# A PEER kernel: the fourth block of 128 tokens by fetched expert rows, the late low halves of u on GpSimd

## The chip, the cores and the metric

The kernel runs on one core of one Trainium2 chip. The core has TensorE (PE, with its weight loads shown as PEld), VectorE (DVE), ScalarE (ACT), GpSimd (POOL) and SyncE (SP), which here only issues DMAs. The metric is the device time of one execution in microseconds. It was measured in three runs, and one more execution was profiled.

## The reference

512 tokens of width 1024, one layer, all in float32. A layer norm, an adaptive modulation (six vectors from `c @ ada_w + ada_b`), a mixer (windowed means and a gated linear recurrence) and a residual come first. Then PEER, a layer of 16384 experts, each with a row of `u` and a row of `v` of width 1024, from which every token picks 128:

```python
def peer(h, w_q, k1, k2, u, v):
    ...
    v1, i1 = lax.top_k(s1, PEER_TOPK)            # 16 of 128 keys, 8 heads
    v2, i2 = lax.top_k(s2, PEER_TOPK)
    ...
    vs, j = lax.top_k(cand, PEER_TOPK)           # 16 of the 256 sums
    e = i1[j // 16] * PEER_NKEYS + i2[j % 16]    # the expert's number
    g = jax.nn.softmax(vs, axis=-1)
    ...
        act = jax.nn.gelu(jnp.einsum('td,tkd->tk', xb, u[eb]))
        return jnp.einsum('tk,tkd->td', gb * act, v[eb])
```

The indexing in the line of `e` is shortened here. A gated residual and a last layer norm follow.

## The kernel before

**PEER is computed densely.** The experts are worked in 128 tiles of 128, for all 512 tokens. For a tile, *expert inputs* are `gelu(u . h)` of 128 experts by 512 tokens; they are multiplied by a gate array that is zero where a token did not pick the expert; then the *values*, gated inputs times `v`, are summed over all tiles into 512 x 1024 outputs. Every float32 product is made of three fast ones from a high and a low half of each operand (`thrice`, lines 1042, 1043 and 1044: high x high, low x high, high x low). ScalarE rounds the high halves (`u_hi`, `v_hi`, `w_hi`), and VectorE or GpSimd subtracts them for the low ones (`u_lo`, `v_lo`, `w_lo`). An input tile is 8 chunks of the width x 3 = 24 matmuls with 512 moving columns.

**The stages.** After the mixer (to some 310 us of the profile) come:
- the *rank stage*: VectorE runs `route`, the top-16 searches for each head (lines 1660 to 1720), while TensorE makes input tiles 0 to 27 (`T_RANK`), with low halves by GpSimd (`split_u`, line 619), between which GpSimd does the affine part of a layer norm (lines 570 and 573). At its end TensorE transposes the routing results (line 1238);
- the *scatter*: 32 steps (`STEPS`, TB x 2 x 4). In each VectorE makes two pairs of one-hot arrays (lines 1760 and 1766), TensorE multiplies them in float16 into gate columns (lines 1249 and 1251) which ScalarE evicts and SP stores to DRAM (`gates`). 20 input tiles (`T_SCATTER`) are made between, low halves by VectorE (line 1753);
- the *store stage*: 16 more input tiles (`T_STORE`) while the last gates are stored. VectorE multiplies the last two pieces of `ada_w` (10 and 11, `partial_modulation`, lines 1396 and 1399). Low halves are GpSimd's. These 64 early tiles are spilled to DRAM (`early`);
- the *late stage*: the values of all tiles and the 64 other input tiles. 30 groups (`group`, `NQ`) of four tiles each: two late input tiles (`late_inputs`, 48 matmuls) and, by Strassen-Winograd's scheme on 2 x 2 blocks, 7 products of 12 matmuls, 84 in all. VectorE makes the sums ahead of it (`value_sums`, `weight_sums`), multiplies by the gates (`weigh`, lines 1793 and 1801), makes low halves (`lo_v`, line 1806, and `lo_w`, line 1811), and adds the products from PSUM into accumulators (`add_up`, line 1816, 11 a group). GpSimd makes the low halves of u in halves of 512 (line 642), each after a wait for a VectorE operation that puts it beside an `add_up`. The last 8 tiles are summed in the 8 banks (`last_sums`);
- the *end*: residual, layer norm (lines 2002 to 2013) and the output DMA.

**What sets the order.** Each engine runs its own queue in the order written. They wait for each other through semaphores by count. SP issues nearly all DMAs in order; a load waits until its buffer is read, so a blocked issue holds those behind it. `u_raw` has four buffers, `u_hi` and `u_lo` two, `v_raw` and `w_raw` four.

## Time and profile before

| | us |
|---|---|
| runs, median (lowest, highest) | 1713.15 (1711.06, 1713.55) |
| profiled execution | 1714.83 |
| its span, first to last instruction | 1713.0 |
| PE busy | 1690.3 (99%) |
| DVE busy | 1533.3 (90%) |
| ACT busy | 770.2 (45%) |
| POOL busy | 392.2 (23%) |
| DMA | 293.22 MB, mean 171 GB/s |

Busy times are sums over the profiled span. They count neither waits nor the issue of DMAs, and matmuls are pipelined, so that their durations overlap: the time that one costs is the distance of the starts of two in a row. The TensorE clock granted was 0.99 of full speed over the span.

### The profile page before, as it was taken

Reading aid. Unit: us, or ns where it says so; the run is one execution under the profiler, and the core shown is the slowest. Engines: PE = TensorE matmul, PEld = TensorE weight load, DVE = VectorE, ACT = ScalarE, POOL = GpSimd, SP = SyncE. Lnnn points to the kernel's source line nnn. Section 1 sums busy time; section 2 is a strip of 40 time slices with the busy share of each in tenths; the row PEclk is TensorE's granted clock in tenths of the full one; section 3 lists DMA queues with packets and bytes.
Section 4 is the critical chain, followed back from the end, with each engine's and each line's share of the span. In section 5 each row is a group of like instructions: output and inputs, shape, how many; then the busy total and the mean of one; then the engine's idle time right before and its main releaser. Section 6 shows DMA issues by size and latency. Waiting matters only on the chain.

```text
span 1713.0 us, 23880 instructions
## 1 busy us (share of the span) xinstructions
PE 1690.3 (99%) x8162; PEld 1369.0 (80%) x8162; DVE 1533.3 (90%) x2332; ACT 770.2 (45%) x843; POOL 392.2 (23%) x248
## 2 busy tenths in 40 slices
PE   8999999999999999999999999999999999999998
PEld 6774688888888888888888888888888888888886
DVE  6988879999899991579999999999999999999998
ACT  1460633323388883344444443534444343444440
POOL 1000345474400003422122222212222122222210
PEclk7999999999999999999999999999999999999999
DMA  9544410245459999744445343444534345443441
GB/s 386 210 165 161 160 46 1 76 140 196 148 176 281 284 285 317 259 164 167 150 148 183 139 177 125 165 166 147 184 122 174 145 150 181 147 180 117 174 179 74
DMA packets 139448, 293.22 MB, mean 171 GB/s; under 512 B 8288, under 2 KB 76000, under 8 KB 136704
## 3 DMA queue, kind: packets, MB, share of 16 engines
q1 hardware_dynamic: 137680, 287.34, 48.0%
q0 software_dynamic: 1424, 4.85, 0.8%
q8 instruction: 34, 0.56, 0.1%
q10 hardware_dynamic: 288, 0.29, 0.1%
q14 instruction: 22, 0.18, 0.0%
HBM read 237.93 MB, written 54.53 MB: 171 GB/s over the span
## 4 chain that ended last, share of the span: by engine, by line
PE 64%; DVE 16%; issue 9%; DMA 6%; POOL 2%; SPq 1%; ACT 1%; DVEq 0%; POOLq 0%; ACTq 0%
PE bank L1042 19%; PE bank L1044 19%; PE bank L1043 19%; DMA w_raw<-early_dram 5%; DVE acc L1816 2%; PE bank L1249 2%; PE bank L1251 2%; DVE v_lo L1806 1%; POOL u_lo L642 1%; DVE u_raw L1840 1%; DVE v_sum L1843 1%; DVE w_raw L1793 1%; DVE arena L1399 1%; PE bank L1128 1%; PE bank L1183 1%
## 5 line engine op out<-in xcount | busy, mean ns | idle before, releaser
L1042 PE MATMUL bank<-h_hi,u_hi 128*128 128x512 f32 x1264 | 498.6, 394 | 1.7 <-POOL u_lo L619 1.7
L1044 PE MATMUL bank<-h_hi,u_lo 128*128 128x512 f32 x1264 | 492.9, 390 | 0.0
L1043 PE MATMUL bank<-h_lo,u_hi 128*128 128x512 f32 x1264 | 492.7, 390 | 0.0
L1042 PE MATMUL bank<-v_hi,w_hi 128*128 128x512 f32 x872 | 341.7, 392 | 1.5 <-DVE acc_p L1816 1.3
L1043 PE MATMUL bank<-v_lo,w_hi 128*128 128x512 f32 x872 | 339.5, 389 | 0.0
L1044 PE MATMUL bank<-v_hi,w_lo 128*128 128x512 f32 x872 | 339.4, 389 | 0.0
L642 POOL TENSOR_TENSOR u_lo<-u_raw,u_hi 128x512 fp32r<-128x512 f32 x120 | 156.1, 1302 | 622.1 <-DVE w_raw L1793 417.0
L1042 PEld LDWEIGHTS bank<-h_hi,u_hi 128*128 128x128 f32 x1264 | 237.6, 188 | 50.7 <-issue 2.0
L1044 PEld LDWEIGHTS bank<-h_hi,u_lo 128*128 128x128 f32 x1264 | 237.7, 188 | 50.4
L1043 PEld LDWEIGHTS bank<-h_lo,u_hi 128*128 128x128 f32 x1264 | 237.9, 188 | 49.0 <-issue 0.7
L1042 PEld LDWEIGHTS bank<-v_hi,w_hi 128*128 128x128 f32 x872 | 163.7, 188 | 42.9 <-DVE acc_p L1816 8.9
L1044 PEld LDWEIGHTS bank<-v_hi,w_lo 128*128 128x128 f32 x872 | 163.7, 188 | 34.3
L1043 PEld LDWEIGHTS bank<-v_lo,w_hi 128*128 128x128 f32 x872 | 163.7, 188 | 33.1
L619 POOL TENSOR_TENSOR u_lo<-u_raw,u_hi 128x1024 fp32r<-128x1024 f32 x45 | 113.5, 2523 | 309.0 <-ACT u_hi L823 309.0
L885 ACT ACTIVATE v_hi<-v_raw 128x2048 fp32r<-128x2048 f32 x62 | 118.5, 1912 | 116.9 <-PE bank L1044 116.9
L1806 DVE TENSOR_TENSOR v_lo<-v_raw,v_hi 128x2048 fp32r<-128x2048 f32 x62 | 152.9, 2466 | 12.5 <-DMA early_dram<-arena 6.3
L1816 DVE TENSOR_TENSOR acc<-acc,bank 128x512 f32<-128x512 f32 x240 | 153.3, 679 | 0.5 <-PE bank L1044 0.5
L912 ACT ACTIVATE w_raw<-bank 128x512 f32<-128x512 f32 x64 | 38.3, 599 | 226.9 <-PE bank L1044 134.8
L830 ACT ACTIVATE arena<-bank 128x512 f32<-128x512 f32 x64 | 38.9, 608 | 165.9 <-PE bank L1044 165.9
L889 ACT ACTIVATE w_hi<-w_raw 128x1024 fp32r<-128x1024 f32 x62 | 65.9, 1064 | 81.2 <-PE bank L1044 79.9
L1801 DVE TENSOR_TENSOR w_raw<-w_raw,gate_in 128x1024 f32<-128x1024 f32 x31 | 38.6, 1247 | 46.0 <-DMA w_raw<-early_dram 45.9
L1811 DVE TENSOR_TENSOR w_lo<-w_raw,w_hi 128x1024 fp32r<-128x1024 f32 x62 | 78.9, 1272 | 0.0
(259 smaller groups left out, 2383.1 us busy)
## 6 DMA issues: line engine op xcount, KB each, us to landing
u_raw<-ut_dram SPq DMA_DIRECT2D x128, 512.0 KB, 3.5
v_raw<-v_dram SPq DMA_DIRECT2D x128, 512.0 KB, 6.3
gate_in<-gates_dram SPq DMA_DIRECT2D x64, 512.0 KB, 5.1
...
```

Of the source, the lines that this page charges most:

```text
L619: pool.tensor_tensor(u_lo[:, c % GT], u_raw[:, c % RT], u_hi[:, c % GT].bitcast(F32), ALU.subtract).then_inc(s_ulo, 1)
L642: return pool.tensor_tensor(u_lo[:, j, k], u_raw[:, 2 + j, k], u_hi[:, j, k].bitcast(F32), ALU.subtract)
L830: act.activation(gelu_out[:, c % GT, :], bank[banks[c % GT]][:, :], ACT.Gelu_apprx_tanh).then_inc(s_act, 1)
L885: act.activation(slots(v_hi, a, b), made, ACT.Copy).then_inc(s_vhi, 1)
L889: act.activation(slots(w_hi, a, b), made, ACT.Copy).then_inc(s_whi, 1)
L1042: pe.matmul(out, a_hi, b_hi, start=(k == 0), stop=False)
L1043: pe.matmul(out, a_hi, b_lo, start=False, stop=False)
L1044: return pe.matmul(out, a_lo, b_hi, start=False, stop=(k == n - 1))
L1801: ve.tensor_tensor(made, made, gate_in[:, :, :, 0, :], ALU.mult).then_inc(s_w, 1)
L1806: ve.tensor_tensor(slots(v_lo, a, b), made, slots(v_hi, a, b).bitcast(F32), ALU.subtract).then_inc(s_vlo, 1)
L1811: ve.tensor_tensor(slots(w_lo, a, b), made, slots(w_hi, a, b).bitcast(F32), ALU.subtract).then_inc(s_wlo, 1)
L1816: ve.tensor_tensor(part, part, bank[b][:, :], ALU.add).then_inc(s_acc, 1)
```

## The change

**Tokens.** Only three of the four blocks of 128 tokens (`DENSE = 3`) are worked densely. An input tile has 384 moving columns (`SD`), the scatter 24 steps, the gates 6 stages (`NST`). The mixer and the routing are still done for all 512 tokens.

**Values.** Winograd's scheme goes. Each tile has 6 outputs (3 blocks x 2 halves of the width) x 3 = 18 matmuls of 512 columns, which accumulate in banks 0 to 5 over the whole late stage; there is no `add_up`. The loop goes by pairs of tiles: one late input tile, then 36 value matmuls; 60 pairs, then three input tiles, then two closing passes of 72 matmuls.

**The fourth block.** For each of the 128 picks GpSimd fetches one row per token by an indirect DMA (128 rows of 4 KB, 512 KB), of u for picks 0 to 127 and of v for 128 to 255, into six row buffers (`first_rows`, 2, and `quad`, 4). VectorE multiplies each with `h_nat`, the block's h in natural layout, and sums along the row; after a gelu and the gates (at pair 28) it multiplies the rows of v with the pick's weight and adds them into `picked`. 12 picks stand in the store stage, then four in each pair. `h_nat` comes from 16 small f32 matmuls in the store stage.

**Low halves.** In the store stage VectorE makes those of u (tiles 52 to 65), in the late stage GpSimd, whole (128x1024) and between its fetches.

**Early tiles.** Still 64, as 36 + 16 + 12. `ada_w` 10 is loaded ahead of the scatter, into `xt`; 11 after it, into `quad`.

```diff
+DENSE = TB - 1
+SD = DENSE * P
+XB = TB - 1
-STEPS = TB * 2 * 4
+STEPS = DENSE * 2 * 4
-T_TURN, T_RANK, T_SCATTER, T_STORE = 27, 28, 5 * TB, 16
+T_TURN, T_RANK, T_SCATTER, T_STORE = 35, 36, 16, 12
```

SyncE's queue in the store stage:

```diff
-                if s in LATE_ADA:
-                    sp.wait_ge(s_scmm, 4 + S // 4)
+                if s == LATE_ADA_AT:
+                    sp.wait_ge(s_scmm, 4 + SD // 4)
+                    sp.dma_start(late_ada[1], ada_w[11]).then_inc(s_late[1], 16)
```

GpSimd's new function and its late loop:

```diff
+            def fetch(n):
+                of, k = (u, v_rows)[n // PICKS], n % PICKS
+                if n >= NBUF:
+                    pool.wait_ge(s_used, n - NBUF + 1)
+                pool.indirect_dma_start(row_buf(n), None, of, bass.IndirectOffsetOnAxis(ap=pick_at[:, k:k + 1], axis=0)
+                                        ).then_inc(s_rows_of[n % NBUF], 16)
...
+            for c in range(-1, PER * LOOPS):
+                n = first + (c + 1) * SLOT_PAIRS
+                for m in range(n, n + SLOT_PAIRS // 2):
+                    if m < 2 * PICKS:
+                        fetch(m)
+                split_u(0, T_EARLY + c + 3)
+                for m in range(n + SLOT_PAIRS // 2, n + SLOT_PAIRS):
+                    if m < 2 * PICKS:
+                        fetch(m)
```

TensorE's late loop:

```diff
+            def pair(i, c):
+                expert_inputs(i, T_EARLY + c + 1, BANKS_SCATTER[(c + 1) % 2], i * RT + (T_EARLY + c))
+                pe.wait_ge(s_wlo, i * PER + (c + 1))
+                pe.wait_ge(s_vlo, i * PER + (c + 1))
+                for j in range(2):
+                    w_of, v_of = pair_of(c % 2, j)
+                    for t in range(DENSE):
+                        for half in range(2):
+                            mm = values(w_of, v_of, t, half, isinstance(i, int) and i + c + j == 0, False)
```

VectorE's picks, and their places in `prepare(c)`:

```diff
+            def picks(count):
+                for n in range(done[0], done[0] + count):
+                    k, rows_of = n % PICKS, row_buf(n)
+                    ve.wait_ge(s_rows_of[n % NBUF], 16 * (n // NBUF + 1))
...
+                        ve.scalar_tensor_tensor(out=rows_of, in0=rows_of, scalar=1.0, in1=h_nat[:, :], op0=ALU.mult,
+                                                op1=ALU.mult, accum_out=dots[:, k:k + 1]).then_inc(s_used, 1)
...
+                    ve.scalar_tensor_tensor(out=picked[:, :], in0=rows_of, scalar=pick_g[:, k:k + 1], in1=picked[:, :],
+                                            op0=ALU.mult, op1=ALU.add).then_inc(s_used, 1)
...
+                else:
+                    picks(one)
+                    lo_v(c + 1)
+                    picks(one)
+                weigh(c + 1)
+                picks(2 * one)
+                lo_w(c + 1)
```

**Orders, before and after.** GpSimd, from the end of its rank loop to the first group of the late stage, before (u_lo are low halves of u, xcount operations in a row):

```order
L628 COMPARE_AND_BRANCH
L619 TENSOR_TENSOR u_lo<-u_raw,u_hi 128x1024 x19
L659 MEMSET acc 128x2048
L642 TENSOR_TENSOR u_lo<-u_raw,u_hi 128x512 x4
L655 TENSOR_TENSOR w_lo<-row_b,w_hi 128x2x256
```

GpSimd in the late stage, after (L586 is `split_u`, L609 `fetch`):

```order
L609 DMA quad<-u_dram,pick_at 128x1024 x2
L609 DMA first_rows<-u_dram,pick_at 128x1024 x2
L586 TENSOR_TENSOR u_lo<-u_raw,u_hi 128x1024
L609 DMA quad<-u_dram,pick_at 128x1024 x4
L586 TENSOR_TENSOR u_lo<-u_raw,u_hi 128x1024
L609 DMA first_rows<-u_dram,pick_at 128x1024 x2
L609 DMA quad<-u_dram,pick_at 128x1024 x2
```

The whole low halves now stand between fetches, two ahead and two behind each.

VectorE in the store stage, before: the last low half of the scatter, then the two pieces of `ada_w` (L1396, L1399):

```order
L1753 TENSOR_TENSOR u_lo<-u_raw,u_hi 128x1024
L1396 TENSOR_SCALAR arena<-acc,sc 128x512
L1399 SCALAR_TENSOR_TENSOR arena<-acc,sc,arena 128x512 x7
L1863 MEMSET acc 128x2048
L1865 MEMSET row_g 128x1024
L1396 TENSOR_SCALAR arena<-arena,sc 128x512
L1399 SCALAR_TENSOR_TENSOR arena<-arena,sc 128x512 x7
L1414 TENSOR_TENSOR row_gate<-row_gate,bank 128x512 x2
L1870 MEMSET acc_p 128x512
```

The same place, after (L1645 is `split_u`, L1282 and L1285 are the pieces, piece 10 in `xt`, piece 11 in `quad`):

```order
L1645 TENSOR_TENSOR u_lo<-u_raw,u_hi 128x1024 x2
L1282 TENSOR_SCALAR arena<-xt,sc 128x512
L1285 SCALAR_TENSOR_TENSOR arena<-xt,sc,arena 128x512 x3
L1645 TENSOR_TENSOR u_lo<-u_raw,u_hi 128x1024
L1285 SCALAR_TENSOR_TENSOR arena<-xt,sc,arena 128x512 x4
L1746 MEMSET picked 128x1024
L1645 TENSOR_TENSOR u_lo<-u_raw,u_hi 128x1024
L1282 TENSOR_SCALAR arena<-quad,sc 128x512
L1285 SCALAR_TENSOR_TENSOR arena<-quad,sc,arena 128x512 x3
L1645 TENSOR_TENSOR u_lo<-u_raw,u_hi 128x1024
L1285 SCALAR_TENSOR_TENSOR arena<-quad,sc,arena 128x512 x4
L1645 TENSOR_TENSOR u_lo<-u_raw,u_hi 128x1024 x4
```

The low halves of u have moved here from GpSimd, and two of them stand between and behind the parts of piece 11.

VectorE in the first group of the late stage, before (L1840 to L1845 `value_sums`, L1829 to L1834 `weight_sums`):

```order
L1840 TENSOR_TENSOR u_raw<-v_raw 128x2x512
L1842 TENSOR_TENSOR v_raw<-v_raw 128x2x512
L1843 TENSOR_TENSOR v_sum<-v_raw,u_raw 128x1024
L1845 TENSOR_TENSOR u_raw<-v_raw,v_sum 128x2x512
L1793 TENSOR_TENSOR w_raw<-w_raw,gate_in 128x512
L1816 TENSOR_TENSOR acc<-acc,bank 128x512 x2
L1829 TENSOR_TENSOR row_b<-w_raw 128x2x256
L1831 TENSOR_TENSOR w_raw<-w_raw 128x2x256
L1832 TENSOR_TENSOR w_sum<-row_b,w_raw 128x512
L1834 TENSOR_TENSOR row_b<-w_raw,w_sum 128x2x256
L1816 TENSOR_TENSOR acc<-acc,bank 128x512 x2
L1806 TENSOR_TENSOR v_lo<-v_raw,v_hi 128x2x1024
```

The same stage, after (L1688 `lo_v`, L1707 a pick, L1683 `weigh`, L1694 `lo_w`), the first pair and the start of the next:

```order
L1707 SCALAR_TENSOR_TENSOR first_rows,dots<-first_rows,h_nat 128x1024
L1688 TENSOR_TENSOR v_lo<-v_raw,v_hi 128x2048
L1707 SCALAR_TENSOR_TENSOR first_rows,dots<-first_rows,h_nat 128x1024
L1683 TENSOR_TENSOR w_raw<-w_raw,gate_in 128x768
L1707 SCALAR_TENSOR_TENSOR quad,dots<-quad,h_nat 128x1024 x2
L1694 TENSOR_TENSOR w_lo<-w_raw,w_hi 128x2x384
L1707 SCALAR_TENSOR_TENSOR quad,dots<-quad,h_nat 128x1024
```

The sums and the operations that read the banks are gone; picks stand between what is left.

## Rows read from the trace of the kernel before

**Rows 1.** Busy time by stage: window, us; engine busy (instructions); PE clock; DMA share; GB/s.
```profile
310.00:464.00 154.00, 152.30 (x685) 126.29 (x686) 149.54 (x549) 50.27 (x64) 88.07 (x36) 0.99 0.43 146
472.00:643.00 171.00, 169.58 (x1485) 142.32 (x1485) 166.29 (x146) 150.52 (x165) 0.00 (x0) 1.00 0.85 258
643.00:742.00 99.00, 99.00 (x441) 81.31 (x439) 37.23 (x31) 35.37 (x43) 42.91 (x17) 1.00 0.78 273
742.00:1680.00 938.00, 936.54 (x4110) 769.25 (x4109) 882.72 (x933) 410.39 (x376) 196.64 (x152) 1.00 0.44 157
```

**Rows 2.** Timeline, late stage, TensorE and weight loads: start, duration, operation.
```profile
1188.31 0.39 PE L1044 MATMUL bank<-v_hi,w_lo 128*128 128x512 f32 x1
1188.54 0.39 PE L1042 MATMUL bank<-v_hi,w_hi 128*128 128x512 f32 x1
1188.54 0.19 PEld L1043 LDWEIGHTS bank<-v_lo,w_hi 128*128 128x128 f32 x1
```

**Rows 3.** Timeline, plain f32 matmuls of 512 and of 384 columns, TensorE.
```profile
179.73 7.11 PE L1128 MATMUL bank<-wbuf,arena 128*128 128x512 f32 x16
186.68 0.49 PE L1015 MATMUL bank<-cst 128*128 128x384 f32 x1
186.68 3.39 PE L1015 MATMUL bank<-cst 128*128 128x384 f32 x10
```

**Rows 4.** VectorE groups: operation, shapes xcount | busy us, mean ns | idle before.
```profile
L1806 DVE TENSOR_TENSOR v_lo<-u_raw,v_hi 128x2048 fp32r<-128x2048 f32 x29 | 66.1, 2279 | 0.0
L1811 DVE TENSOR_TENSOR w_lo<-w_raw,w_hi 128x1024 fp32r<-128x1024 f32 x62 | 78.9, 1272 | 0.0
L1801 DVE TENSOR_TENSOR w_raw<-w_raw,gate_in 128x1024 f32<-128x1024 f32 x31 | 38.6, 1247 | 46.0 <-DMA w_raw<-early_dram 45.9
L1992 DVE SCALAR_TENSOR_TENSOR u_raw<-u_raw,acc 128x1024 f32<-128x1024 f32 x3 | 3.6, 1221 | 0.0
```

**Rows 5.** GpSimd groups, then a DMA of its queue: KB each, us to landing.
```profile
L619 POOL TENSOR_TENSOR u_lo<-u_raw,u_hi 128x1024 fp32r<-128x1024 f32 x45 | 113.5, 2523 | 309.0 <-ACT u_hi L823 309.0
L553 POOL DMA_DIRECT2D row_b<-rows_dram x2 | 1.1, 538 | 0.0
gate_in<-rows_dram POOLq DMA_DIRECT2D x2, 512.0 KB, 4.9
```

**Rows 6.** Timeline of GpSimd, then of VectorE, rank stage.
```profile
357.42 2.47 POOL L619 TENSOR_TENSOR u_lo<-u_raw,u_hi 128x1024 fp32r<-128x1024 f32 x1 [0.68 <-ACT u_hi L823]
...
357.55 2.42 DVE L1703 SCALAR_TENSOR_TENSOR arena<-arena 128x64 f32<-128x64 uint32 x1
362.38 1.23 DVE L1707 TENSOR_TENSOR arena<-arena,cst 128x1024 f32<-128x1024 f32 x1
...
370.21 3.41 DVE L1712 TENSOR_TENSOR arena<-arena 128x1024 f32<-128x1024 f32 x1
```

**Rows 7.** Timeline of VectorE, one and a half scatter steps.
```profile
562.62 2.36 DVE L1766 TENSOR_TENSOR acc<-acc,arena 128x2048 f16<-128x2048 f16 x2
564.89 1.23 DVE L1753 TENSOR_TENSOR u_lo<-u_raw,u_hi 128x1024 fp32r<-128x1024 f32 x1
566.03 2.36 DVE L1760 TENSOR_TENSOR arena<-arena 128x2048 f16<-128x2048 f16 x2
```

**Rows 8.** Timeline: the transposes ahead of the scatter; an ada_w piece, issued and used.
```profile
463.85 1.47 PE L1238 MATMUL bank<-cst,arena 128*128 128x128 f32 x12
...
669.77 0.49 SPq L474 DMA_DIRECT2D acc<-ada_w_dram  x1
...
679.30 0.49 DVE L1396 TENSOR_SCALAR arena<-acc,sc 128x512 f32<-128x512 f32 x1 [36.17 <-DMA acc<-ada_w_dram]
```

**Rows 9.** Busy time, clock, DMA share and GB/s of two stretches.
```profile
800.00:900.00 100.00, 99.99 (x439) 81.91 (x438) 94.95 (x100) 46.85 (x42) 22.08 (x17) 1.00 0.44 158
190.00:200.00 10.00, 7.89 (x44) 7.20 (x44) 8.20 (x16) 7.11 (x11) 1.53 (x3) 0.83 0.98 412
```

**Rows 10.** Timeline of TensorE: its last product.
```profile
1705.14 0.39 PE L1044 MATMUL bank<-h_hi,u_lo 128*128 128x512 f32 x1
```

More of the change, by code:

```diff
@@ new lines, in _ @@
+            pool.wait_ge(s_stage[0], 16 * (DENSE + 1))
+            for n in range(2):
+                fetch(n)
+            pool.wait_ge(s_part, 12)
+            first = NBUF + U_EARLY
+            for n in range(2, first):
+                fetch(n)
+            for c in range(-1, PER * LOOPS):
[7 more added lines that the diff above has]
+                        fetch(m)
@@ new lines, in _ @@
+                if n == FIRST_HI:
+                    act.wait_ge(s_stage[1], 16 * (DENSE + len(LAST_STORE)))
+                    hi_v(0, 0)
+            act.wait_ge(s_stage[0], 16 * (DENSE + 1))
+            late_gelu(0, 0)
+            hi_u(0, T_EARLY + 2)
+            hi_w(0, 0)
+            for c in range(PER):
+                prepare(0, c)
+            with act.Fori(1, AT_GELU) as i:
+                for c in range(PER):
+                    prepare(i, c)
+            act.wait_ge(s_used, PICKS)
@@ L1355, in _, with values @@
-            pe.wait_ge(s_wlo, 4 * NQ + 2 + TAIL)
-            pe.wait_ge(s_vlo, 4 * NQ + 2 + TAIL)
-            for o in range(OUTS):
-                last_sums(o, range(TAIL, 2 * TAIL)).then_inc(s_vmm, 1)
+            def values(w_of, v_of, t, half, first, last):
+                (wh, wl), (vh, vl) = w_of, v_of
+                t, d = slice(t * P, (t + 1) * P), slice(half * DH, (half + 1) * DH)
+                o = 2 * (t.start // P) + half
+                return thrice(bank[o][:, :], 0 if first else 1, 2 if last else 3, ((wh[:, t], wl[:, t]), (vh[:, d], vl[:, d])))
@@ new lines, in _ @@
+            expert_inputs(0, T_EARLY, BANKS_SCATTER[0], T_EARLY - 1)
+            pe.wait_ge(s_hnat, 2)
+            pe.wait_ge(s_rowg, 4)
+            for c in range(PER):
+                pair(0, c)
+            with pe.Fori(1, LOOPS) as i:
+                for c in range(PER):
+                    pair(i, c)
+            for c in range(PER * LOOPS + 1, NGROUP):
+                expert_inputs(0, T_EARLY + c, BANKS_SCATTER[c % 2], T_EARLY + c - 1)
+            pe.wait_ge(s_wlo, NGROUP - CLOSE)
@@ new lines, in _ @@
+            ve.wait_ge(s_rows, 96)
+            evict(0)
+            evict(1)
+            final_times_gain(x_last, XB, 0)
+            evict(2)
+            final_output(x_last, XB, 0)
+            for o in range(3, OUTS):
+                evict(o)
+            ve.wait_ge(s_evict, OUTS)
+            ve.wait_ge(s_xb, 16)
+            link(ve.scalar_tensor_tensor(out=x_back[:, 0:DENSE, :], in0=x_back[:, 0:DENSE, :], scalar=ALPHA,
+                                         in1=quad[:, 0:DENSE, :], op0=ALU.mult, op1=ALU.add))
@@ L1998, in _ @@
+            for tb in range(DENSE):
                 for half in range(2):
```

824 lines of the change are left out of this document (292 added, 532 removed).

## Prediction

> **What bounds the kernel now.** I read first the busy times by stage [rows 1]: in the rank, scatter, store and late stages TensorE is busy 152.3 of 154, 169.6 of 171, 99.0 of 99 and 936.5 of 938 us. TensorE bounds all of it, with VectorE close behind in three stages (149.5, 166.3, 882.7) and free only in the store stage (37.2). Then TensorE's timeline [rows 2]: one product of 128x512 follows the last after .227 us; the weight load takes .19 us and runs beside the product before. So time falls with the number and width of matmuls, until VectorE, GpSimd or the DMA is later.
>
> The sum is made against the profiled execution: span 1713.0 us, run 1714.83, so 1.8 us lie around the span. The median shown, 1713.15, is 0.1% lower.
>
> **The change, part by part.**
>
> *1. Width of an input tile.* 24 matmuls per tile go from 512 to 384 columns. The only rows at both widths are plain f32 [rows 3]: 16 of 512 columns fill 6.95 us (.434 each), then 10 of 384 take 3.39 us, (3.39 - .49)/9 = .322 each: a ratio of .742. For the fast products that gives .168; with some fixed cost I take **.172**, 24 x .172 = 4.13 us per tile against 5.44. Low end .160; high ends .19, if the weight load [rows 2] sets the pace, and .227, no gain.
>
> *2. Values.* Winograd's 84 products per four tiles become 36 per pair, accumulated in six banks: 36 x .227 = 8.16 us. TensorE does slightly fewer (2304 against 2712 in all), and VectorE loses the 0.68 us evictions and the pre-additions.
>
> *3. Rank stage.* Routing is still done for all 512 tokens, so VectorE (149.5 of 154) bounds it; 35 narrow tiles give 35 x 4.13 = 145 us of cover where 27 x 5.44 = 147 did. No gain. GpSimd makes eight more low halves here (2.4 us each [rows 5]), and [rows 6] show what one does to VectorE: an operation of ~.2 us took 2.42 beside one, one of 1.23 took 3.41. Eight cost 0 to 8 x 2.35 = 19 us; I take 8, since many of the routing's operations are short ones with one input and pass. TensorE's transposes, at 463.85 [rows 8], come at about 472, the first scatter product at 480, 8 later than the 472 of [rows 1].
>
> *4. Scatter.* 24 steps, not 32. VectorE's operations there are 1.135 us apart [rows 7]: four, and per step 16/24 of a low half of 1.14 plus up to .3 of waiting. Before: 171.2/32 = 5.35 per step with 20/32 of one; now 5.39. 24 x 5.39 = 129.4, end at 609.4. TensorE needs 1.9 + .667 x 4.13 = 4.7 per step (1.9 is what is left of 5.3 after .625 x 5.44), so VectorE is the bound by itself, and .7 us per step, 17 in all, of what TensorE saves is lost here.
>
> *5. Store stage.* From 609.4: 13 input tiles 53.7; the natural copy of h for the fourth block, 16 small f32 matmuls at the .12 of [rows 8] (12 in 1.47), 1.9; 4 f32 products of the modulation at .434 [rows 3] 1.7; one more tile before the first value product 4.1. **An added wait:** the last piece of ada_w may be loaded only once the scatter is done, and VectorE now waits for it in order, with its low halves of tiles 56 and later queued behind and TensorE behind these. In the trace such a piece was issued at 669.77 and read at 679.30, 9.5 us [rows 8]. Issue two tiles, some 10 us, after the scatter, landing at 19.5 (up to 31, if the gate stores at 78% DMA share [rows 1] go first), then 4.1 + 1.2 on VectorE; TensorE has four tiles and h's copy as cover, 18.4 us. Stall 7 to 18, I take 13, plus 1.7 for the clock: in 190 to 200, where TensorE was busy only 7.9 of 10, the granted clock was .83 [rows 9], 10 x .17. Values start at 609.4 + 76.1 = 685.5.
>
> *6. Late stage.* A pair costs TensorE 4.13 + 8.16 = **12.3 us**. 60 pairs of values 489.6, 62 further input tiles 256.1, 144 closing products 32.7, and the tail from the last product at 1705.14 [rows 10] to the span's end, 7.8: 786.2. The new row work must hide beside it:
> VectorE per pair: low half of v 2.28, gates on 768 columns .75 x 1.25 = .94, low half of w .75 x 1.27 = .95, four picks at 1.22 (as a scalar-tensor-tensor over 128x1024, [rows 4]) 4.88. Sum 9.05. GpSimd's low half locks it for up to 2.35 [rows 6], since nearly all of these operations read two SBUF tensors; before, the late low halves stood beside operations that read PSUM. 11.4 of 12.3.
> GpSimd per pair: 2.4 + 4F, F being one fetch of 128 rows. No trace row has such a fetch. Low end: a plain 128-row issue at .54 [rows 5]. I take twice that, 1.1, which leaves GpSimd at 6.8. The high end is open; F decides from (12.3 - 2.4)/4 = 2.5 on.
> DMA per pair: seven pieces of 512 KB (two of v, one of u, four fetched) are 3.67 MB, gates and early inputs .59 more: 4.26 MB. In the late stage 158 GB/s went with a share of .44, so 359 at a full one; the best stretch moved 412 [rows 9]. That is 11.9 or 10.3 us, also under 12.3. The DMA will be busy nearly all the time: this is the thinnest cover beside VectorE's.
>
> On the fetches the Trainium skill has two rules that no row here shows. SBUF — State Buffer, "Who interferes with whom": an instruction of GpSimd that only writes SBUF is not blocked by VectorE's two-input operations; by it the four fetches add nothing to VectorE's 11.4. DMA: Bandwidth & Descriptors, "Anatomy of one DMA — SWDGE (gpsimd) path": a transfer takes 2.0 us plus its bytes at 436 GB/s: 3.2 us for a fetch, an estimate; were GpSimd held for that long, the pair would take 15.2 us and the run 1652.
>
> *7. The end.* The fourth block is finished during the closing products; its final operations (1.3 us each) are under them. Nothing.
>
> **Sum.** 685.5 + 786.2 = 1471.7; losses like the 1.5 in 938 [rows 1] add 1.2; around the span 1.8: **1475 us**, 14% under 1713.
>
> **The rivals.** Each us per pair costs 61 us.
> A, the forecast: TensorE still bounds the late stage. For it: even with VectorE at 94% TensorE lost only 1.5 us [rows 1]. 1440 (.160 per matmul, no loss in the rank stage) to 1520 (19 and 18 in parts 3 and 5, and 0.4 per pair). Chance .60.
> B, VectorE and GpSimd pace each other, each pair 13 to 15.5 us: the lock plus waits in a fixed order, or fetches of 2.6 to 3.3 us, or a hold of .3 to 1 us on VectorE for each. Typical +1.5 per pair: 1475 + 92 = 1567. One form of it has GpSimd held until the rows have landed, with the run near the bound of E or beyond it; a 512 KB transfer of GpSimd's queue landed 4.9 us after its issue, but the issue took only .54 [rows 5], so I give this form .02. For it: [rows 6], and that 11.4 of 12.3 has no room for a wait; against: GpSimd's low halves are made a tile or two ahead. In all .14.
> C, the DMA is late, scattered rows moving slower than whole tiles: at 300 GB/s 14.2 us per pair, 1475 + 116 = 1591; at 330, 12.9, 1512. For it the 359 of [rows 9], against it the 412. .09.
> D, 384 columns do not go at three quarters: at .19, .018 x 24 x 126 = 54, 1529; at .227, 166, 1641. [rows 3] speak against it, but the weight load of .19 for it. .07.
> E, **slower than before**: GpSimd's fetch. The gain of 240 us is gone when a pair takes 12.3 + 240/61 = 16.2 us, that is F = (16.2 - 2.4)/4 = 3.5 us. At F = 4.5 a pair takes 20.4 and the run 1969. Place: GpSimd's queue of the late stage, where the low half stands behind two fetches, so that a slow fetch also holds TensorE's next input tile. The .54 of [rows 5] speaks against it, though that issue needs no list of rows. .10.
> Beside these, the change may not do what it says: the low half on GpSimd takes 2.4 us of lock from VectorE where VectorE itself would take 1.14 [rows 7]. Then it relieves nothing; but while TensorE bounds the time stays 1475, so this has no chance of its own.
>
> **How the numbers follow.** The forecast is A's 1475. The range, 1440 to 1610, takes in A, C, the lower half and more of B, and D's first case; outside are E (.10), and of B, C and D about .08. A measurement of this kernel can tell about 0.2% from no change. Faster .60 + .14 + .09 + .07, less .01 for B or C ending on 1713: .89; same .01; slower .10.
>
> **What would show it.** Right: TensorE over 97% busy from 690 us on, 24 narrow products in 4.1 us, a pair in 12.3; scatter of about 129 us with VectorE full; one stall of 7 to 18 us in the store stage, released by a chain that starts at ada_w; GpSimd about 55% busy with fetches near 1.1. Wrong: the late idle of TensorE released by GpSimd's low half (B, E), by VectorE's low halves or picks with durations over 2 us (B), picks that wait for rows with the DMA share at 1 (C), or products of 384 columns .19 apart or more (D).

## The result and the profile after

The changed kernel takes **1501.49 us** (median of 4 runs, 1500.03 to 1505.95), the kernel before, beside it, 1712.11. The ratio is 0.8775, 95% interval 0.8753 to 0.8798: 12.3% faster, within the range and 26 us above the forecast of 1475. The profiled execution took 1505.95 with a span of 1504.1. It was the slowest of the four, 4.5 us above the median, and what is read from it below holds that much of the spread between executions.

Lines of the page after: busy times, then by 40 slices of the span the granted clock, the DMA's share and its GB/s.

```profile
span 1504.1 us, 20739 instructions
PE 1443.3 (96%) x7527; PEld 1247.7 (83%) x7527; DVE 1307.6 (87%) x1950; ACT 584.0 (39%) x689; POOL 707.2 (47%) x407
...
PEclk8899999999999999988999999999999999999999
DMA  9734340024655698999999999999999999999961
GB/s 384 253 154 168 140 185 1 1 78 149 215 168 205 222 287 251 333 321 395 368 341 343 341 341 336 345 340 343 339 347 343 338 333 353 342 336 334 351 216 58
```

GpSimd went from 23% to 47%, and the DMA's share is 9 in nearly every late slice, where [rows 1] had .44 for the late stage. By stage (the same columns as [rows 1]):

```profile
310.00:474.00 164.00, 157.32 (x889) 151.25 (x888) 161.00 (x562) 59.04 (x80) 109.77 (x43) 0.99 0.49 162
482.00:613.00 131.00, 117.45 (x1139) 107.92 (x1138) 126.10 (x111) 111.38 (x126) 0.00 (x0) 0.99 0.86 263
613.00:700.00 87.00, 69.94 (x390) 68.31 (x389) 52.83 (x66) 29.70 (x39) 30.50 (x22) 0.90 0.98 347
700.00:1460.00 760.00, 758.92 (x3642) 664.49 (x3643) 659.71 (x541) 253.98 (x243) 501.13 (x297) 1.00 0.94 338
```

These are the rank, scatter, store and late stages. TensorE still fills the late stage (758.9 of 760 us). It no longer fills the scatter (117 of 131, VectorE 126), as part 4 said, nor the store stage: 69.9 of 87 us with a mean granted clock of .90, where [rows 1] had 99.0 of 99 at 1.00.

**The pair.** ScalarE rounds w once in each pair. Two of these rows, 45 pairs apart:

```profile
805.99 0.85 ACT L864 ACTIVATE w_hi<-w_raw 128x768 fp32r<-128x768 f32 x1 [0.69 <-DVE w_raw L1683]
...
1367.64 0.85 ACT L864 ACTIVATE w_hi<-w_raw 128x768 fp32r<-128x768 f32 x1 [0.74 <-DVE w_raw L1683]
```

(1367.64 - 805.99)/45 = **12.48 us** for a pair, against 12.3 forecast. TensorE's timeline shows where the .19 is. The first two rows are an input tile's, the others value products:

```profile
1202.33 0.33 PE L960 MATMUL bank<-h_hi,u_lo 128*128 128x384 f32 x1
1202.51 0.33 PE L958 MATMUL bank<-h_hi,u_hi 128*128 128x384 f32 x1
...
1205.10 0.39 PE L958 MATMUL bank<-v_hi,w_hi 128*128 128x512 f32 x1
1205.33 0.39 PE L959 MATMUL bank<-v_lo,w_hi 128*128 128x512 f32 x1
1205.56 0.40 PE L960 MATMUL bank<-v_hi,w_lo 128*128 128x512 f32 x1
1205.80 0.39 PE L958 MATMUL bank<-v_hi,w_hi 128*128 128x512 f32 x1
```

The narrow products are .173 to .174 apart, as forecast (.172): 384 columns do cost three quarters, as in [rows 3]. The wide ones are not .227 apart as in [rows 2]: .23, .23 and .24 in turn, in the mean of the starts between 1100 and 1300 us .229, .229 and .235, together .231. The slow step is the one from the product with the weights w_lo to the next.

**VectorE and GpSimd in one pair**, VectorE first:

```profile
1201.01 2.29 DVE L1688 TENSOR_TENSOR v_lo<-v_raw,v_hi 128x2048 fp32r<-128x2048 f32 x1 [1.47 <-ACT v_hi L849]
1203.22 1.28 DVE L1715 SCALAR_TENSOR_TENSOR picked<-quad,pick_g,picked 128x1024 f32<-128x1024 f32 x1
...
1205.29 4.62 DVE L1715 SCALAR_TENSOR_TENSOR picked<-quad,pick_g,picked 128x1024 f32<-128x1024 f32 x2
...
1200.66 0.94 POOL L609 DMA_INDIRECT quad<-v_dram,pick_at  x1 [0.30 <-issue]
1204.77 1.41 POOL L609 DMA_INDIRECT quad<-v_dram,pick_at  x1 [3.17 <-DVE picked L1715]
1206.19 2.63 POOL L586 TENSOR_TENSOR u_lo<-u_raw,u_hi 128x1024 fp32r<-128x1024 f32 x1
1208.98 1.75 POOL L609 DMA_INDIRECT quad<-v_dram,pick_at  x1 [0.16 <-issue]
```

The low half of v begins after a wait of 1.47 us for ScalarE's v_hi, which waits for TensorE: this is VectorE's slack in a pair. The two picks at 1205.29 took 4.62 us instead of 2 x 1.28, beside GpSimd's low half at 1206.19: the lock of [rows 6], once per pair. A fetch (DMA_INDIRECT) takes .94 us when VectorE is idle or waits, 1.41 to 1.75 in these rows beside it.

**The store stage.** SyncE's issue of the last ada_w piece; VectorE's first use, and the low half behind it; TensorE's next input tile; then VectorE's two picks and its low half of w at the first pair, and TensorE's first value product:

```profile
628.09 4.11 SPq L466 DMA_DIRECT2D quad<-ada_w_dram  x1
...
641.83 0.49 DVE L1282 TENSOR_SCALAR arena<-quad,sc 128x512 f32<-128x512 f32 x1 [13.41 <-DMA quad<-ada_w_dram]
642.35 2.33 DVE L1285 SCALAR_TENSOR_TENSOR arena<-quad,sc,arena 128x512 f32<-128x512 f32 x3
644.71 1.22 DVE L1645 TENSOR_TENSOR u_lo<-u_raw,u_hi 128x1024 fp32r<-128x1024 f32 x1
...
645.99 0.69 PE L958 MATMUL bank<-h_hi,u_hi 128*128 128x384 f32 x1 [9.52 <-DVE u_lo L1645]
...
695.63 1.22 DVE L1707 SCALAR_TENSOR_TENSOR quad<-quad,h_nat 128x1024 f32<-128x1024 f32 x1
696.78 3.37 DVE L1707 SCALAR_TENSOR_TENSOR quad<-quad,h_nat 128x1024 f32<-128x1024 f32 x1
...
700.08 0.95 DVE L1694 TENSOR_TENSOR w_lo<-w_raw,w_hi 128x768 fp32r<-128x768 f32 x1
...
701.08 0.80 PE L958 MATMUL bank<-v_hi,w_hi 128*128 128x512 f32 x1 [8.62 <-DVE w_lo L1694]
```

Issued at 628.09, 15 us after the last scatter product (612.7), the piece was read at 641.83, 29 us after it. TensorE sat idle for 9.52 us. Later two picks stand between the first pair's gates and its w_lo in VectorE's queue, one of them 3.37 us long beside GpSimd's low half, and TensorE was idle for 8.62 us once more. Both times it restarted at half clock (.69 us for a narrow product, .80 for a wide one that takes .39 in [rows 2]).

### The profile page after: what moved, and what is told of

Read it like the earlier page. It is cut to its first block, busy times and chain, and to the rows that moved or that the text cites. A ratio compares the mean times of both kernels' runs of the same rounds, so it can differ in the third digit from the quotient of the medians.

```text
span 1504.1 us, 20739 instructions
## 1 busy us (share of the span) xinstructions
PE 1443.3 (96%) x7527; PEld 1247.7 (83%) x7527; DVE 1307.6 (87%) x1950; ACT 584.0 (39%) x689; POOL 707.2 (47%) x407
## 4 chain that ended last, share of the span: by engine, by line
PE 62%; DVE 28%; DMA 3%; ACT 3%; issue 2%; SPq 0%; POOL 0%; DVEq 0%; ACTq 0%
PE bank L960 19%; PE bank L959 19%; PE bank L958 19%; DVE arena L1556 2%; DVE arena L1548 2%; DVE arena L1598 1%; DVE arena L1553 1%; DVE arena L1545 1%; DVE arena L1652 1%; DVE arena L1594 1%; DMA early_dram<-arena 1%; DVE arena L1285 1%; DVE arena L1550 1%; DVE arena L1597 1%; DVE u_lo L1645 1%
## 5 line engine op out<-in xcount | busy, mean ns | idle before, releaser
L958 PE MATMUL bank<-h_hi,u_hi 128*128 128x384 f32 (+1 forms) x1256 | 442.8, 353 | 17.3 <-DVE u_lo L1645 9.5
L959 PE MATMUL bank<-h_lo,u_hi 128*128 128x384 f32 (+1 forms) x1256 | 435.2, 347 | 0.0
L960 PE MATMUL bank<-h_hi,u_lo 128*128 128x384 f32 (+1 forms) x1256 | 435.2, 347 | 0.0
L586 POOL TENSOR_TENSOR u_lo<-u_raw,u_hi 128x1024 fp32r<-128x1024 f32 x98 | 253.5, 2587 | 85.7 <-ACT u_hi L784 84.6
L959 PEld LDWEIGHTS bank<-h_lo,u_hi 128*128 128x128 f32 x1256 | 238.0, 189 | 12.3 <-issue 0.7
L1688 DVE TENSOR_TENSOR v_lo<-v_raw,v_hi 128x2048 fp32r<-128x2048 f32 x62 | 142.2, 2294 | 95.3 <-ACT v_hi L849 93.7
L609 POOL DMA_INDIRECT quad<-u_dram,pick_at x84 | 119.7, 1425 | 112.9 <-DVE quad L1707 63.3
L609 POOL DMA_INDIRECT quad<-v_dram,pick_at x86 | 124.8, 1451 | 90.2 <-DVE picked L1715 69.9
L1715 DVE SCALAR_TENSOR_TENSOR picked<-quad,pick_g,picked 128x1024 f32<-128x1024 f32 x86 | 151.2, 1758 | 2.5
L609 POOL DMA_INDIRECT first_rows<-u_dram,pick_at x44 | 63.9, 1453 | 186.1 <-DMA gates_dram<-wbuf 134.7
L1707 DVE SCALAR_TENSOR_TENSOR quad<-quad,h_nat 128x1024 f32<-128x1024 f32 x84 | 142.4, 1714 | 0.3 <-DMA quad<-u_dram,pick_at 0.3
L784 ACT ACTIVATE u_hi<-u_raw 128x1024 fp32r<-128x1024 f32 x128 | 134.7, 1053 | 0.0
```

The source lines that it names most:

```text
L586: pool.tensor_tensor(u_lo[:, c % GT], u_raw[:, c % RT], u_hi[:, c % GT].bitcast(F32), ALU.subtract).then_inc(s_ulo, 1)
L609: pool.indirect_dma_start(row_buf(n), None, of, bass.IndirectOffsetOnAxis(ap=pick_at[:, k:k + 1], axis=0)).then_inc(s_rows_of[n % NBUF], 16)
L784: act.activation(u_hi[:, c % GT], u_raw[:, c % RT], ACT.Copy).then_inc(s_uhi, 1)
L958: pe.matmul(out, a_hi, b_hi, start=(k == 0), stop=False)
L959: pe.matmul(out, a_hi, b_lo, start=False, stop=False)
L960: return pe.matmul(out, a_lo, b_hi, start=False, stop=(k == n - 1))
```

## The experiments

The theory after the result: TensorE bounds the late stage, and fetches, picks, lock and DMA are hidden under it; the time over the forecast comes mostly from the store stage and from the .231. The rivals: VectorE paced by the lock, a fetch's cost on GpSimd, the DMA near its limit. In all profiles the pair, and the time from the first value product to the last product, can be read apart from the stages ahead. That matters, for these vary by themselves: the transposes begin between 470.0 and 475.3 us in kernels that are the same up to there, and from the last scatter product to the first value product the kernels that leave this stretch alone take 83.1 (e9), 85.2 (e11), 85.5 (e8), 86.4 (e5), 87.6 (e12) and 88.3 us (the changed kernel).

### The low halves of u on VectorE (e1_split_vector)

The call goes from GpSimd's loop, where it stood between fetches, to VectorE's `prepare(c)`:

```diff
                 weigh(c + 1)
+                split_u(0, T_EARLY + c + 3)
                 picks(2 * one)
                 lo_w(c + 1)
```

> VectorE, not GpSimd, makes the late low halves of u (between the gates and the third pick of each pair). Theory (the late stage is bound by TensorE, 12.5 us a pair; VectorE waits 1.5 us of it for v_hi): no change of the time, within 0.3% of the changed kernel's 1501.5 us; VectorE's busy time per pair falls from 10.9 to about 9.8 us (the lock's 2.2 us go, 1.14 come), no pick longer than 1.3 us, and the fetches get shorter or stay. Rival (the lock or GpSimd's order costs TensorE time): 5 to 12 us faster. Other rival (VectorE in a fixed order holds the low half too late): slower by 10 us or more.

Measured: 1499.78 us (1497.83 to 1500.74), ratio to before 0.8753 (0.8732 to 0.8774): not told apart from the changed kernel. The stretch 800 to 1400, its busy times and the picks, first of the changed kernel, with its GpSimd groups:

```profile
800.00:1400.00 600.00, 600.00 (x2888) 525.15 (x2887) 520.86 (x418) 203.14 (x194) 404.15 (x241) 1.00 0.95 341
...
L1715 DVE SCALAR_TENSOR_TENSOR picked<-quad,pick_g,picked 128x1024 f32<-128x1024 f32 x76 | 132.3, 1741 | 2.2
...
L586 POOL TENSOR_TENSOR u_lo<-u_raw,u_hi 128x1024 fp32r<-128x1024 f32 x48 | 124.9, 2601 | 0.8
L609 POOL DMA_INDIRECT quad<-v_dram,pick_at x80 | 116.6, 1458 | 82.7 <-DVE picked L1715 63.4 <-issue 15.8 <-DVE quad L1707 3.3
```

and with the low halves on VectorE:

```profile
800.00:1400.00 600.00, 600.00 (x2886) 525.07 (x2885) 477.39 (x465) 202.65 (x194) 284.93 (x193) 1.00 0.96 342
...
L1713 DVE SCALAR_TENSOR_TENSOR picked<-quad,pick_g,picked 128x1024 f32<-128x1024 f32 x76 | 97.3, 1280 | 2.2
```

VectorE is busy 477 instead of 521 us of 600, although it does more; picks fell from 1741 to 1280 ns. The pair stays at 12.48. So the change takes 1.22 us per pair (the low half in e1) off VectorE's program and gives 2.1 us back by the lock: GpSimd as the place of the low halves costs VectorE .9 us of a pair ((521 - 477)/48 pairs) and TensorE nothing. The forecast said that it relieves nothing, and that this has no price as long as TensorE bounds.

### Fetches of 8 elements (e2_short_rows) and picks of 8 columns (e3_short_picks)

e2, from the seventh fetch on:

```diff
-                pool.indirect_dma_start(row_buf(n), None, of, bass.IndirectOffsetOnAxis(ap=pick_at[:, k:k + 1], axis=0)
+                pool.indirect_dma_start(row_buf(n)[:, 0:8], None, of.rearrange('n (a b) -> (n a) b', b=8), bass.IndirectOffsetOnAxis(ap=pick_at[:, k:k + 1], axis=0)
```

e3 (the picks of v likewise):

```diff
-                        ve.scalar_tensor_tensor(out=rows_of, in0=rows_of, scalar=1.0, in1=h_nat[:, :], op0=ALU.mult,
+                        ve.scalar_tensor_tensor(out=rows_of[:, 0:8], in0=rows_of[:, 0:8], scalar=1.0, in1=h_nat[:, 0:8], op0=ALU.mult,
```

> From the seventh on, each fetch brings 8 elements of a row (32 bytes) instead of 1024, still 128 rows by an indirect DMA; VectorE's picks keep their size (the dots are multiplied by zero so that numbers stay finite). The fourth block's output is therefore not the reference's. It takes 2.1 MB per pair from the DMA and leaves GpSimd's and VectorE's work. Theory (TensorE bounds the late stage; the DMA's 4.26 MB per pair are hidden): a pair stays at 12.4 to 12.5 us, DMA share about .5, time within 5 us of the changed kernel apart from the store stage. Rival (scattered rows on the DMA slow TensorE's products from .227 to .231 or hold VectorE): a pair falls to 12.3, -12 us.

> VectorE's picks work on 8 columns instead of 1024; the fetches are whole. The fourth block's output is not the reference's. It takes 4.6 us of work and with it nearly all lock encounters from VectorE in each pair. Theory: a pair stays at 12.45 to 12.5 us, VectorE busy about 5 of it, fetches all near .94 to 1.7 us; up to 10 us faster, all of it ahead of the first value product. Rival (VectorE's chain paces the pair): 12.3 or less, -12 us or more.

Measured: 1498.32 us (two runs) and 1494.93 (two runs, 1490.74 to 1499.12). Columns as above, 800 to 1400, of e2:

```profile
800.00:1400.00 600.00, 600.00 (x2886) 525.02 (x2885) 521.75 (x415) 202.17 (x193) 407.38 (x241) 1.00 0.53 175
```

and of e3, with GpSimd's low halves and fetches:

```profile
800.00:1400.00 600.00, 600.00 (x2886) 525.12 (x2885) 332.30 (x414) 202.34 (x194) 318.41 (x241) 1.00 0.93 341
...
L586 POOL TENSOR_TENSOR u_lo<-u_raw,u_hi 128x1024 fp32r<-128x1024 f32 x49 | 117.8, 2404 | 4.1 <-ACT u_hi L784 0.5 <-issue 0.2
L609 POOL DMA_INDIRECT quad<-v_dram,pick_at x80 | 82.0, 1025 | 121.9 <-DVE picked L1715 104.6 <-issue 12.3 <-DVE quad L1707 5.0
```

Without the fetched bytes the DMA's share falls from .95 to .53, and the pair is 12.48 as before. Without the picks VectorE is busy 332 instead of 521 of 600, and the pair is 12.48 as before. Neither the DMA nor VectorE nor the lock has a part in it, and the .231 stays with both. Nor does the length of a row count on GpSimd: over this stretch a fetch takes 1.47 us in the mean in e2 (32 bytes a row) and 1.45 in the changed kernel (4096). In e3 the fetches of the last row fall from 1458 to 1025 ns: most of what a fetch costs above .94 is waiting for VectorE. The Trainium skill (SBUF — State Buffer, "Who interferes with whom") says that a VectorE operation with two SBUF inputs contends with a GpSimd instruction that reads SBUF. A fetch reads its 128 row numbers (`pick_at`) from there, and its .5 to .8 us of waiting agree with that. The other direction, a fetch that holds VectorE up, does not occur: in e1, without GpSimd's low halves, the 63 picks of v that overlap a fetch take 1282 ns in the mean and the 65 others 1279.

### Twice the fetches (e4_twice_small)

```diff
+                pool.indirect_dma_start(spare8[:, 8 * (n % NBUF):8 * (n % NBUF) + 8], None, of.rearrange('n (a b) -> (n a) b', b=8), bass.IndirectOffsetOnAxis(ap=pick_at[:, k:k + 1], axis=0)
+                                        ).then_inc(s_rows_of[n % NBUF], 16)
-                    ve.wait_ge(s_rows_of[n % NBUF], 16 * (n // NBUF + 1))
+                    ve.wait_ge(s_rows_of[n % NBUF], 32 * (n // NBUF + 1))
```

> Each fetch is followed by a second one of 8 elements per row into a spare place, and the pick waits for both: GpSimd's queue doubles at nearly the same DMA bytes. It prices a fetch on GpSimd. From the changed kernel's rows (.94 alone, 1.42 to 1.75 beside VectorE, .30 between two, 2.6 the low half) a pair needs 8 x 1.45 + 8 x .3 + 2.6 = 16.6 us of GpSimd. Theory (the slower case of the prediction is real, its point just not reached): the pair goes to 14.5 to 17 us, 1625 to 1775 us. Rival (a fetch costs GpSimd .94 and the rest of its row is waiting that overlaps): 8 x 1.24 + 2.6 = 12.5, no change.

Measured: 1694.58 us (1686.17 and 1702.98), ratio to before 0.9893 (0.9772 to 1.0013): 13% over the changed kernel, and not told apart from the kernel before. A pair takes 15.6 us. GpSimd's timeline (L609 the fetch, L611 the small one, L586 the low half), then a wait of TensorE:

```profile
1200.97 0.95 POOL L611 DMA_INDIRECT gap<-v_dram,pick_at  x1 [0.30 <-issue]
1201.95 2.38 POOL L586 TENSOR_TENSOR u_lo<-u_raw,u_hi 128x1024 fp32r<-128x1024 f32 x1
1204.49 1.76 POOL L609 DMA_INDIRECT quad<-v_dram,pick_at  x1 [0.16 <-issue]
...
1208.62 0.94 POOL L609 DMA_INDIRECT quad<-v_dram,pick_at  x1 [0.31 <-issue]
...
1218.00 2.36 POOL L586 TENSOR_TENSOR u_lo<-u_raw,u_hi 128x1024 fp32r<-128x1024 f32 x1
...
1204.46 0.44 PE L960 MATMUL bank<-h_hi,u_hi 128*128 128x384 f32 x1 [1.44 <-POOL u_lo L586]
```

Here GpSimd has no idle time left but the .30 between two, 16 us from one low half to the next. Of TensorE's 86.8 us idle between 800 and 1400 us its low half of u ended 58.3; VectorE's w_lo, behind picks that wait for the small fetches, ended 27.6. So the slower case of the prediction is a real mechanism. Eight issues per pair cost (15.6 - 2.4)/8 = 1.65 us each, .30 between two included; a single fetch per pick would have to cost (15.9 - 2.4)/4 = 3.4 us to lose the whole gain (12.48 + 209/61 = 15.9, 209 being the difference of the spans), and costs 1.45 + .30 = 1.75.

### Half a megabyte more per pair (e8_more_dma)

```diff
+                if late:
...
+                    sp.dma_start(gap3[:, c % 2 * 1024:c % 2 * 1024 + 1024], v[bass.ds(i * 8 + 2 * c, 1)].rearrange("a p n -> p (a n)")
+                                 ).then_inc(s_more[c % 2], 16)
```

> SyncE loads one more tile of v (512 KB) per pair into a spare place: 4.78 MB per pair instead of 4.26; nothing reads it. It prices the DMA's slack. Theory (the DMA moves 359 to 412 GB/s at a full share; at 94% share a pair has .7 us left): a pair needs 4.78/.360 = 13.3 us or 11.6 at .412; TensorE waits for loads, 13.0 to 13.5 us a pair, 1530 to 1565. Rival (the share of .94 has slack that shrinks under pressure, packets are only slower because they overlap): a pair stays at 12.5, 1501.

Measured: the profiled execution took 1500.61 us. A second run took 3659.77; nothing here tells why, and it is left aside. 800 to 1400:

```profile
800.00:1400.00 600.00, 600.00 (x2886) 525.09 (x2885) 521.74 (x418) 202.84 (x194) 403.80 (x241) 1.00 1.00 384
```

384 GB/s at a share of 1.00, and the pair is 12.48 as before. The theory fell: a share of .95 at 341 GB/s does not mean that 5% is left. The share counts the time that packets take, and it overstated how near the limit was. The rate at a share of .44, scaled to 1 (359), was no bound; the saturated stretch of [rows 9] (412) was the better guide. This rests on one execution.

### Where the operands of a product lie (e5_order, e9_layout_w, e11_gap768, e12_aligned)

In e5 only the order of the three value parts is changed, in the others only the unused places between tensors. e9 puts gap1 (720 elements) ahead of w_hi and not behind it; e12 puts 24 elements ahead of w_hi, with gap1 704 and gap2 808. e5's order, which only the value products use, and e11's gaps:

```diff
+            def thrice_b(out, k, n, pairs):
...
+                pe.matmul(out, a_hi, b_hi, start=(k == 0), stop=False)
+                pe.matmul(out, a_lo, b_hi, start=False, stop=False)
+                return pe.matmul(out, a_hi, b_lo, start=False, stop=(k == n - 1))
...
-        sb("gap1", [P, 720])
+        sb("gap1", [P, 768])
...
-        sb("gap2", [P, 816])
+        sb("gap2", [P, 768])
```

> In the value products the three parts are ordered high x high, low weights x high, high weights x low; nothing else changes. In the changed kernel the start of the product after high x high (same weights w_hi, v_lo next) comes .236 us later, the two others .229. Theory A (it is the reload of the same weights, or the weight array's place): the slow step changes its place with the weights, mean stays .231 or falls to .229, up to 5 us faster. Theory B (it is the moving v_hi stream beside the load of w_hi): one slow step stays, time within 2 us.

> Only w_hi's place in SBUF is changed, by 2880 bytes. The products of v and w come .231 us apart in the late stage and in the first closing pass, those of the second closing pass, whose operands lie elsewhere, .227. Theory (the place of the operands costs 4 ns per product): the mean changes, to .227 at best, -9 us. Rival (it is something else in that stage): mean .231, no change.

> Only w_lo's place in SBUF moves, by 192 bytes (gap1 768 elements instead of 720, gap2 768 instead of 816). Counted in elements from the first tensor, each rounded up to 8, w_hi stands at 33064 and w_lo at 35320: remainders 40 and 56 by 64; in the kernel before both were 40, and so are u_hi and u_lo; in e9_layout_w both were 56. The spacing of the products was .231, .227, .227 (second closing pass) and .2333. Theory (a weight array at remainder 56 costs the products around its load 4 to 6 ns): with both at 40 the mean is .227, a pair 12.33 us, 9 us faster, about 1492. Rival (it is w_hi's place alone, or the distance to v): .231, 1501.

> w_hi and w_lo both at remainder 0 (33088 and 35328). Theory (only 56 is bad, 0 is at least as good as 40): spacing .227 or less, 1490 to 1493. Rival (each distance to the moving array matters, not the remainder): .229 or more, 1497 or more.

Measured (places in elements, their remainder by 64; spacing as the mean of starts between 1100 and 1300 us):

| | w_hi | w_lo | value products apart | pair, us | time, us | ratio to before (95%) |
|---|---|---|---|---|---|---|
| changed kernel | 40 | 56 | .231 | 12.48 | 1501.49 | 0.8775 (0.8753 to 0.8798) |
| e5_order | 40 | 56 | .231 | 12.48 | 1498.87 | 0.8760 (0.8735 to 0.8784) |
| e9_layout_w | 56 | 56 | .233 | 12.58 | 1505.48 | 0.8789 (0.8718 to 0.8860) |
| e11_gap768 | 40 | 40 | .228 | 12.39 | 1495.01 | 0.8725 (0.8708 to 0.8742) |
| e12_aligned | 0 | 0 | .234 | 12.62 | 1508.98 | 0.8800 (0.8781 to 0.8820) |

The same stretch, 800 to 1400, of e9, e11 and e12 in turn. TensorE is busy all the time in each; what differs is how many products it did (behind the x):

```profile
800.00:1400.00 600.00, 600.00 (x2865) 520.76 (x2864) 516.44 (x413) 201.33 (x192) 399.22 (x239) 1.00 0.94 339
```

```profile
800.00:1400.00 600.00, 600.00 (x2905) 529.70 (x2905) 525.73 (x420) 203.07 (x194) 410.33 (x243) 1.00 0.96 344
```

```profile
800.00:1400.00 600.00, 600.00 (x2857) 521.89 (x2856) 514.84 (x415) 201.53 (x193) 397.98 (x238) 1.00 0.94 338
```

2865, 2905 and 2857 (the changed kernel: 2888). That the place of the stationary arrays moves the pace is shown: nothing else was touched, and e11 and e12 lie apart by more than their intervals. A move of w_lo by 192 bytes is worth .09 us of a pair, and from the first value product to the last product 792.7 us become 786.6.

TensorE's products in e5:

```profile
1200.82 0.39 PE L965 MATMUL bank<-v_hi,w_hi 128*128 128x512 f32 x1
1201.05 0.40 PE L966 MATMUL bank<-v_hi,w_lo 128*128 128x512 f32 x1
1201.29 0.39 PE L967 MATMUL bank<-v_lo,w_hi 128*128 128x512 f32 x1
1201.52 0.39 PE L965 MATMUL bank<-v_hi,w_hi 128*128 128x512 f32 x1
```

The expectation of e5 names the wrong step for the changed kernel: there the product after high x high comes .229 later, and the .235 follow the product with w_lo. With the order changed the slow step still follows that product (.234, the others .230 and .229). So it goes with w_lo, as theory A had it. e11, which moves only w_lo, takes it away (.229, the others .227 and .228); e9, which moves only w_hi, from 40 to 56, makes the other two slow too (.233, .233, .234). Up to there the remainder 56 looked like the cause. That only 56 is bad fell with e12: 0 is the worst of the four. Which relation between the places of stationary and moving arrays counts stays open; v_hi and v_lo are at remainder 40 throughout, as are both in the kernel before, and equal remainders were the best of the four layouts. Even e11 is .001 above [rows 2].

### The store stage (e6_ada_behind, e7_first_w) and all together (e10_all)

e10 has e11's gaps, e1's low halves, e7's order, and piece 11 at 4 and 5 with `AT_GATE2` at 8. The edits of e6 (the other half of the piece goes from 3 to 7, `AT_GATE2` from 6 to 9) and of e7, in VectorE's `prepare`:

```diff
-                if n == 2:
+                if n == 6:
                     partial_modulation(11, range(KD // 2))
...
+                if c == -1:
+                    lo_v(0)
+                    weigh(0)
+                    lo_w(0)
+                    picks(4 * one)
+                    return
```

> Piece 11 of ada_w is multiplied four tiles later in VectorE's queue (behind the low half of tile 59 instead of 55), and TensorE's modulation three tiles later. Theory (the 9.5 us idle of TensorE at 646 and its slower clock around it come from the low halves queued behind that wait): that idle goes; but the fetches into quad and the gates' load wait for piece 11 too, so part of it comes back before the first value product: 5 to 12 us faster, 1490 to 1497. Rival (the store stage is bound by the DMA, share .98): the idle only moves, within 2 us of 1501.5.

> The first pair's gates and low halves of v and w are made ahead of the four picks of that step instead of between them. Theory (TensorE's 8.6 us idle at 692 to 701 is VectorE being late with w_lo behind four picks, one of them locked to 3.4 us): the first value product comes 3 to 5 us earlier, 1496.5 to 1498.5. Rival (it is the DMA of v or gates that is late): no change.

> Together: w_lo's place as in e11_gap768; late low halves of u by VectorE; the first pair's gates and low halves ahead of its picks; piece 11 of ada_w two tiles later in VectorE's queue (modulation two tiles later). Theory (the gains lie in different places: 9 us in the late stage, 9 to 12 between the scatter and the first value product): 1478 to 1484. Rival (the store stage is bound by the DMA, so that its gains don't add): 1484 to 1490.

Measured: e6 1496.04 us (ratio 0.8738, 0.8717 to 0.8759), e7 1495.05 (0.8735, 0.8713 to 0.8757), e10 1490.89 (0.8689, 0.8667 to 0.8711). From the last scatter product to the first value product the profiles show 83.2 us in e6, 79.1 in e7 and 77.8 in e10, and 83.1 to 88.3 in the kernels that leave this stretch alone. So e7 and e10 gain there clear of the spread; e6 does not, and by its time, too, it cannot be told from e1 and e5, which ran beside it (1499.78 and 1498.87; their intervals overlap e6's). e7's is below the range that was expected, but its interval overlaps e5's as well.

e6's 9.5 us idle is gone, and four idles (7.4 us in all) stand in its place. The longest, 3.6 us, ends behind picks that waited for fetches into quad, which wait for piece 11 too; one of 1.9 ends behind the multiplication by the piece and two picks. The two others, 2.0 us, come before the piece is used; the longer of them, 1.7, stands behind ScalarE, which waited 3.8 us for early inputs to be stored (`early_dram`). e10's waits of TensorE from 600 us on (us in all, times, longest):

```profile
PE bank L956 <- DVE u_lo L1643: 5.1, 3, 2.3
PE bank L956 <- DVE w_lo L1692: 4.5, 2, 2.8
```

Of the 18.1 us of such idle in the changed kernel 9.6 are left. Here the rival of e6 and e10, the DMA, has a part: the longest of the idles behind u_lo, 2.3 us, follows a low half that began at 673.09 after 6.00 us of waiting for ScalarE's u_hi, and ScalarE had waited 6.27 us for an early tile's inputs to be stored; in the changed kernel the DMA's share is .98 in this stage. e10 is the fastest kernel here, 0.7% below the changed one by the medians, with intervals of the ratios that lie apart, and 13.1% below the kernel before, but it missed both its expectations (1478 to 1490): the 6 us of the layout and 10 us of the store stage add up to 1485, and 1491 was measured. Between the two profiled executions the difference is 14.3 us: 10.6 ahead of the first value product and 4.1 from there to the last product (6.2 in e11), less .4 at the end. But the changed kernel's profiled execution lay 4.5 us above its median, so gains read from it promise too much when they are taken off the median. Against e11, with the same layout, the rest of e10 brings 4.1 us by the medians, with intervals that still overlap.

## Why the prediction was right, and where it was off

The direction, the mechanism and the range held: TensorE bounds the late stage. Point by point, against the profiled span of 1504.1 (forecast 1472.9, the sum of 1471.7 and 1.2; by the medians the miss is 26 us and not 31):

1. **Width.** .172 forecast, .1733 measured: 4.16 us per tile for 4.13. The ratio of the plain products in [rows 3] could be carried over, and the weight load of .19 did not stand in the way.
2. **Values.** .227 forecast, .231 measured: the mis-sized term. With the .001 of the narrow products it makes 12.48 per pair for 12.29 (4.13 + 8.16), 60 x .19 = 11.4 us. I took the spacing of [rows 2] for a property of the product's shape; it is one of shape and place, as e11 and e12 show. The first 5.7 us of the values (701.1 to 706.8), at a granted clock of half speed after the idle, add 2.7, and the closing products about .2.
3. **Rank stage.** Transposes at 472 forecast, 474.8 measured (470.0 to 475.3 among the profiles). Against the kernel before that is 10.9 us later, where the sum had 8 and the range 0 to 19. VectorE is busy 161.0 us there instead of 149.5, which fits the lock; no run takes the eight low halves away, so this cause is argued and not shown. The first scatter product came 7.6 us behind the transposes, for 8.
4. **Scatter.** 129.4 us forecast, 482.4 to 612.7 = 130.3 measured, bound by VectorE.
5. **Store stage.** 76.1 forecast, 88.3 measured (83.1 to 88.3 in kernels that leave it alone). The wait for ada_w cost TensorE 9.5 us, where the sum had 13. That it came near is in part luck: the piece landed 29 us after the scatter, for 19.5, but TensorE had 23.7 us of other work as cover, for 18.4. Four things were mis-sized. Three quarters of the scatter's last input tile come after its last product and stand in no term (3.1 us). h's natural copy is 32 products, not the 16 of the description of the change, for h_hi and h_lo are both transposed (3.5 us, not 1.9). The clock, granted at half speed from 638.55 to 652.21, cost about 3 us, for 1.7, since TensorE was idle in the first part of that time. And I had costed at nothing the 12 picks and the first pair's low halves in VectorE's queue, ahead of the first value product, though they were in the order of operations that I quoted. That wait was 8.6 us (5.3 to 8.6 in kernels with this order); in e7, by one reordering, two idles of 4.2 us in all are left of it.
6. **Late stage beside TensorE.** VectorE 11.4 us per pair forecast, (521 of 600) x 12.48 = 10.8 measured. GpSimd: F forecast 1.1, measured 1.45, and .30 between two that stood in no term; (404 of 600) x 12.48 = 8.4 busy, 67% for the 55 that were to be seen. DMA: 4.26 MB in 12.48 us are 341 GB/s, as measured.
7. **The end.** 7.8 forecast, 1504.1 - 1493.8 = 10.3 measured, both from the start of the last product [rows 10] (9.4 to 10.7 among the profiles, 11.4 in e4). VectorE was still finishing the block before when TensorE ended and took up the last one at 1495.9, 2 us behind; in the kernel before it had done so at 1704.7, ahead of the last product.

Together 2.8 - .4 for the rank stage, 1.0, 12.2, 11.4 + 2.7 + .2 and 2.5 are 32.4 us; less the 1.2 that stood in the sum for losses, that is the 31.2 by which the span is over the forecast one.

Of the rivals, B did not come: the lock is there as priced, but 1.5 us of slack per pair took it (e1, e3). C did not come either, with more room than I gave it (e2, e8). D is refuted by the rows. E did not come, but its mechanism exists: in e4 GpSimd's queue sets the pair. With what was measured the gain would be gone at 3.4 us per fetch, where the forecast had 3.5; a fetch costs half of that. The Trainium skill (DMA: Bandwidth & Descriptors, "Anatomy of one DMA — SWDGE (gpsimd) path") gives 2.0 us plus the bytes at 436 GB/s for a transfer, by estimate 3.2 us for a fetch, and the prediction asked what would come of it if GpSimd were held for that long. It is not: the row says .94, with rows of 4096 bytes and of 32 (e2, e4).
